# WKV chunk inversion: products of 64x64x64 on the diagonal chunks in place of 128x128x128

## The reference

```python
def direction(dirn):
    wl = (w0[dirn] + jnp.tanh(xw @ w1[dirn]) @ w2[dirn]).astype(F32)
    decay = jnp.exp(-jnp.exp(-jax.nn.softplus(-wl) - 0.5))
    a = jax.nn.sigmoid((a0[dirn] + (xa @ a1[dirn]) @ a2[dirn]).astype(F32))
    kd = kf * (1.0 + (a - 1.0) * k_a.astype(F32))
    ...
    y = wkv7_scan(rf, decay, kd, vf, -kk, kk * a, reverse=(dirn == 1))
```

## Time and profile before

| | |
|---|---|
| median of 3 runs | 3637.33 us (3633.06 to 3642.9) |
| the profiled execution | 3643.23 us, span 3641.4 us |
| TensorE (PE) matmuls | busy 3355.4 us, 92% of the span |
| VectorE, ScalarE, GpSimd | 56%, 40%, 20% of the span |
| mean granted TensorE clock | 0.959 |

### The profile page before, as it was taken

How to read it: one execution, slowest core, us unless ns; L and a number is a source line. 1 busy time by engine, 2 the same in 40 slices (tenths; PEclk the granted TensorE clock), 3 DMA queues, 4 the chain that set the end, 5 groups by cost and what they waited for, 6 DMA issues and landing times. The chain is left out here.

```text
span 3641.4 us, 46010 instructions
## 1 busy us (share of the span) xinstructions
PE 3355.4 (92%) x18440; PEld 2691.7 (74%) x18440; DVE 2047.3 (56%) x2984; ACT 1465.1 (40%) x2418; POOL 727.2 (20%) x496
## 2 busy tenths in 40 slices
PE   8888999999879999989899997969999999979999
PEld 6656787878557888866688875748888888768887
DVE  6665534355764534456566466446666666447554
ACT  5444322334454223334543233445444444324332
POOL 0000302120002202110011012315444444201101
PEclk9989999999889999989999998989999999989999
DMA  4101322222002222210223222440000000023222
GB/s 146 37 1 64 105 97 94 93 81 82 4 36 81 95 97 93 95 58 1 70 94 103 87 98 88 167 164 21 21 24 24 24 24 33 7 81 99 98 88 87
DMA packets 82291, 260.46 MB, mean 72 GB/s; under 512 B 9632, under 2 KB 13216, under 8 KB 81696
## 3 DMA queue, kind: packets, MB, share of 16 engines
q1 hardware_dynamic: 71424, 236.02, 19.9%
q10 hardware_dynamic: 10656, 21.50, 1.6%
HBM read 236.51 MB, written 20.97 MB: 71 GB/s over the span
## 5 line engine op out<-in xcount | busy, mean ns | idle before, releaser
L1634 DVE TENSOR_TENSOR mlp_w_lo<-mlp_ring,mlp_w_hi 128x1024 fp32r<-128x1024 f32 (+1 forms) x211 | 251.6, 1193 | 620.1 <-ACT mlp_w_hi L1614 619.9
L1614 ACT ACTIVATE mlp_w_hi<-mlp_ring 128x1024 fp32r<-128x1024 f32 (+1 forms) x211 | 213.1, 1010 | 711.2 <-PE ps L1575 704.0
L1634 DVE TENSOR_TENSOR ffn_w_lo<-ffn_ring,ffn_w_hi 128x1024 fp32r<-128x1024 f32 (+3 forms) x172 | 225.7, 1312 | 459.7 <-ACT ffn_w_hi L1614 459.7
L1614 ACT ACTIVATE ffn_w_hi<-ffn_ring 128x1024 fp32r<-128x1024 f32 (+3 forms) x172 | 186.9, 1088 | 493.6 <-PE ps L1575 487.3
L1574 PE MATMUL ps<-mlp_more_parts,mlp_w_hi 128*128 128x512 f32 x952 | 378.4, 397 | 0.0
L1573 PE MATMUL ps<-mlp_more_parts,mlp_w_hi 128*128 128x512 f32 x760 | 312.9, 412 | 43.7 <-DVE mlp_w_lo L1634 29.4
L1573 PE MATMUL ps<-tiles_parts,mlp_w_hi 128*128 128x512 f32 x832 | 331.2, 398 | 8.0 <-issue 5.7
L1573 PE MATMUL ps<-ffn_x_parts,ffn_w_hi 128*128 128x512 f32 x792 | 312.6, 395 | 26.3 <-DVE ffn_x_parts L2344 20.9
L1575 PE MATMUL ps<-tiles_parts,mlp_w_lo 128*128 128x512 f32 x832 | 328.6, 395 | 0.0
L1574 PE MATMUL ps<-ffn_x_parts,ffn_w_hi 128*128 128x512 f32 x792 | 309.9, 391 | 0.0
L1575 PE MATMUL ps<-ffn_x_parts,ffn_w_lo 128*128 128x512 f32 x792 | 309.9, 391 | 0.0
(11 more groups left out here) (494 smaller groups left out, 6983.6 us busy)
## 6 DMA issues: line engine op xcount, KB each, us to landing
ffn_ring<-in_w_ffn_up SPq DMA_DIRECT2D x88, 512.0 KB, 3.7
mlp_ring<-in_w_up SPq DMA_DIRECT2D x64, 512.0 KB, 3.7
mlp_ring<-in_w_down SPq DMA_DIRECT2D x64, 512.0 KB, 3.7
rwkv_keep<-ffn_ring ACTq DMA_DIRECT2D x64, 256.0 KB, 2.5
sq<-rwkv_keep SPq DMA_DIRECT2D x64, 256.0 KB, 2.9
ffn_ring<-in_w_ffn_down SPq DMA_DIRECT2D x16, 768.0 KB, 4.4
in_ring<-in_w_in SPq DMA_DIRECT2D x22, 512.0 KB, 3.8
mlp_ring<-in_w_in SPq DMA_DIRECT2D x22, 512.0 KB, 3.7
```

The source lines that it names most:

```text
L1614: nc.scalar.activation(w.w_hi[:, n % SPLIT, 0:width], w.ring[:, n % RING, 0:width], ACT.Copy).then_inc(s["w_hi_ready"], 1)
L1634: nc.vector.tensor_tensor(w.w_lo[:, n % SPLIT, 0:width], w.ring[:, n % RING, 0:width], w.w_hi[:, n % SPLIT, 0:width].bitcast(F32), ALU.sub ...
```

## The change

Each of the four products of an `inner` or an `outer` becomes two, one for each diagonal chunk: rows and columns 0 to 63, and 64 to 127. The off-diagonal quarters are no longer multiplied; those of T1 receive whatever the PSUM bank held, and nothing reads them. The order of the blocks, all waits and all other engines' instructions stay as they are. A block has 8 matmuls in the code in place of 4.

```diff
                     for i in range(4):
-                        mm = nc.tensor.matmul(m.ps[:, t % 2, i * P:(i + 1) * P], NM[:, u % 2, i, :], XT[:, t, i, :], start=True, stop=True)
+                        for chunk in (half(0), half(1)):
+                            at = slice(i * P + chunk.start, i * P + chunk.stop)
+                            mm = nc.tensor.matmul(m.ps[chunk, t % 2, at], NM[chunk, u % 2, i, chunk], XT[chunk, t, i, chunk], start=True, stop=True,
+                                                  skip_group_check=True)
                     mm.then_inc(s["inner_ready"], 1)
...
                     for i in range(4):
-                        mm = nc.tensor.matmul(m.ps[:, 2 + t, i * P:(i + 1) * P], X[:, t, i, :], T1[:, t % 2, i, :], start=False, stop=True,
-                                              skip_group_check=True)
+                        for chunk in (half(0), half(1)):
+                            at = slice(i * P + chunk.start, i * P + chunk.stop)
+                            mm = nc.tensor.matmul(m.ps[chunk, 2 + t, at], X[chunk, t, i, chunk], T1[chunk, t % 2, i, chunk], start=False, stop=True,
+                                                  skip_group_check=True)
                     mm.then_inc(s["outer_ready"], 1)
```

## The result

The changed kernel takes 3588.74 us (median of 4 runs, 3587.22 to 3596.46) against 3636.96 us for the kernel before (4 runs): a ratio of 0.987, 95% interval 0.9851 to 0.989, or 48 us less. It is within 3 us of the rival "the clock holds" (3591), but, as the rows show, the clock did not hold.

What follows compares the result with a forecast made beforehand. TensorE was taken to bound the stage. +7 us for merges at half clock and +26 us behind them gave +33 us: 3676 against the profiled 3643.23, or 3670 from the median's side; range 3590 to 3712.

Steps and rivals of the forecast that it cites:

- the clock holds: Rival for the merges: TensorE's clock stays at 1.00 beyond their first part; 3591 us, chance 0.13.
- The new block at full clock: TensorE's split block in the merge: 16 records at 0.028 us each, 0.44 us in place of 0.89.
- The quarters don't run at once: Rival: diagonal quarters writing the same PSUM bank take turns, blocks of 0.88 us, 1.76 at half clock; about 3915 us, chance 0.08.
- What that would give with the clock as it is: Merge's second part shrinks from 24 us to 17 to 18, first part next to nothing; 46 us over eight iterations: 3591.
- The clock: TensorE's clock falls within the first 3 to 7 us of nearly each merge and doesn't come back in it.
- The merge at half clock: Blocks take 0.88 us and scan steps 5.2 us more; merge 46.9 against 45.9 us, +7 us over seven merges.
- behind the merge: After each merge the clock returns late: 2 us lost, or 10 in one case of six; +26 us over eight.
- The upper end: Slow end of the forecast's case: recovery missed three times in six, block of 0.92 at half clock; +75 us, 3712.

Runs made afterwards that it cites:

- one_chunk: The changed kernel with only chunk 0 of each product computed, chunk 1's inversion left out: 3656.92 us (one run; kernel before beside it 3641.3).
- half_cols: Against the changed kernel, chunk 1's inversion left out; 8 records a block on 128 rows and 64 columns, 128 columns streaming: 3627.52 us (one run).
- half_rows: Against the changed kernel, chunk 1's inversion left out; 8 records a block on 64 rows and 128 columns, 128 columns streaming: 3783.66 us (one run).
- hybrid: Against the kernel before, levels 0 and 1 keep full 128x128x128 products and levels 2 to 4 are split: 3595.76 us, ratio 0.9888.
- grouped: The changed kernel with its two loops exchanged, four products of chunk 0 first, then four of chunk 1: 3618.29 us (one run).

## Why the prediction was wrong

**"The new block at full clock": right.** 0.44 forecast, 0.47 measured; the two quarters run at once (one_chunk: 8 records are as long as the changed kernel's 16). "The quarters don't run at once" fell with it; the rule of the Trainium skill ("TensorEngine Tiling (Array Packing)", Gotcha 1) is not borne out here as a wait: diagonal quarters wrote the same PSUM bank, on different partitions, and 16 records took 0.47 us where one quarter's 8 take 0.46.

**"What that would give with the clock as it is": right in size, by two errors.** I had about 6 us in each of eight merges from the second part, 46 in all. The seven merges before the last gained 4.1 to 5.3 us, the last 11.6 us, because POOL has no work for a next pair there and doesn't pace it (it waits 17.1 us for TensorE); together 45.6, and 1.1 more in the stretches between them. The first part gave nothing, as forecast. That the sum fits is luck: the seven are too high and the last too low, and the falls of the clock are in what was measured.

**"The clock": half right.** It fell in every merge, after waits that were nearly all for POOL, though not in the first 3 to 7 us but after 14 to 18 (in the first merge at 6 and again at 17). The failed step is the next clause: that it would "not come back in it, since nothing in it fills the array any more". It came back in every one, after 3.4 to 10.2 us; in the merge shown after 2645.98 to 2649.40, behind 56 records, nearly all of 64x64 blocks side by side. I had read rows and columns of the array as one share. Of the falls in the earlier trace rows, those after 2541.30 and in 3176.15 to 3200.00 hold records on 64 rows; the one after 298.70 has half-column records, but in pairs side by side, with the engine busy just 1.66 of 3.40 us, and in the one after 2841.60 it was busy 1.71 of 3.46 us, most of it on the full array. I had also read too much into 2541.30: the `update` records that I named have all started by 2542.6, and from 2542.81 to the fall TensorE runs L2740, on the full array with 64 streaming columns. half_cols and half_rows part rows from columns: with unused columns the clock was back after 3.4 us, with unused rows it wasn't until the merge was over. Two diagonal quarters at once use half of the array, but between them every row; one_chunk, which uses 64 rows, stayed down as I had forecast for the changed kernel, at 3657 us.

**"The merge at half clock" and "behind the merge": right terms for a case that didn't come.** A block took 0.85 us against 0.88. one_chunk, whose blocks of 8 in one quarter last as long as those of 16 in two, shows the case itself: its merge is 46.9 us in four of the six iterations in the middle, what I had summed, and from `wt` to the next merge it takes 1.4 or 2.4 us longer than in the changed kernel in four of them and 9.0 us in one, where I had 2 and, in one of six, 10. In the changed kernel `wt` never ran at half clock (2.02 us), so +26 us behind the merge was nothing, and +7 us for the merge was -46.

**Slips in the working.** The merge's first part has 17 blocks, not about 21. The upper end's own terms give about +68 us, not +75, so 3705 and not 3712. Neither bears on the step that failed.

**The rival "the clock holds"** gave the time (3591 against 3589) though the clock didn't hold: PEclk is 0.84 and 0.93 in the merge's parts. What the fall cost is small: 2.5 us for one of 10 us (hybrid's pair), so by estimate at most 20 us for the eight merges. The Trainium skill's tie of the lower clock to gaps ("TensorE: Matmul & The Clock Gate", HAM oscillation) did better here than my reading in that the clock came back with dense work, but half_rows, busy 63.51 of 65.96 us at 0.64, shows that gaps aren't all of it.

**What stays open:** why the second quarter starts only after five records in grouped; which measure of the work brings the clock back, beyond rows not being the same as columns; what the clock alone would give the changed kernel, since hybrid held it in part only; and how much of the last merge's 11.6 us would be there without scan steps, which wasn't tried.

## What to carry to other kernels

A matmul on a block-diagonal matrix can be split into its diagonal quarters: here they ran side by side when their products stood alternately in the queue, and a block fell from 0.89 to 0.47 us. Before forecasting such a gain, look who is next: here POOL took over at once, and halving its masks in turn was worth another two thirds of the gain (3589 to 3558 us). A granted clock seen to fall in one part of a trace says what was going on there, not which property of it mattered; a pair of kernels that differ in that property alone tells them apart. Ask of a fall two questions, what starts it and what ends it: in half_cols and half_rows alike it began at POOL's waits, and the price was set by how long it lasted, 3.4 us or 51.

## What the runs showed that was not expected

- Records on 64 rows and 128 columns: granted clock 0.64 in a merge that was 96% busy; on 128 rows and 64 columns, 0.96. The same 64-row records kept 1.00 through the last merge, 42.0 us, in which the clock hadn't fallen.
- 64x64x64 float32 records: 0.057 us each in one quarter (one_chunk), 0.027 to 0.031 us with the diagonal quarter beside it (0.47 us from one block of 16 to the next).
- The order of eight independent products in a block changed their pace from 0.028 to 0.049 us a record; the second quarter's records began when five of the first's eight had started.
- A merge's length at PEclk 1.00, 0.95 and 0.90 was 31.2, 32.4 and 34.0 us: the fall cost about as much where VectorE was 97% busy as where POOL set the pace.
